# The last quarter of the attention steps: mixed tile, logits, value products, then the newer step's first head; on ScalarE the projection ahead of that head's copy

## The reference, cut to what matters

```
h = rms_norm(x, g_pre) * (1 + scale) + shift
p = h @ w_in            # indexer, retention (4 heads), gates, attention (8 query heads, 2 key/value heads)
mask: for each query the 256 best keys by an indexer's score (80 for the sample)
logits = q . k / 8, masked;  probs = softmax(logits);  o_a = probs @ v
mixed = concat(o_a * silu(gate_a), groupnorm(o_b) * silu(gate_b))
x = x + gate * rms_norm(mixed @ w_out, g_post)
```

## Time and profile before

| | us |
|---|---|
| median of 3 runs | 1493.13 (1491.31 to 1493.81) |
| profiled execution | 1492.05 |
| its span | 1490.2 |
| PE busy | 1392.9 (93%) |
| DVE busy | 1045.6 (70%) |
| ACT busy | 787.5 (53%) |
| POOL busy | 410.3 (28%) |

### The profile page before, as it was taken

One profiled execution on the slowest core, in us unless ns is written; L12 is line 12 of the kernel. 1 busy time (PEld: TensorE's weight loads), 2 busy tenths in 40 slices (PEclk: granted clock), 3 DMA queues, 4 the chain that ended last, 5 costly groups with the idle time before them and its releaser, 6 DMA issues.

```text
span 1490.2 us, 24410 instructions
## 1 busy us (share of the span) xinstructions
PE 1392.9 (93%) x7591; PEld 1060.5 (71%) x7591; DVE 1045.6 (70%) x3021; ACT 787.5 (53%) x1916; POOL 410.3 (28%) x360
## 2 busy tenths in 40 slices
PE   6779999999999999989996999999999999998997
PEld 1655777777887667657885677878887766765885
DVE  1697889999996556542287889999999655654225
ACT  2455666666325655654453566666631656656422
POOL 2551332433331001001188113433333101100100
PEclk9999999999999999999998999999999999999999
DMA  8422333423222112213252111211222211211324
GB/s 303 141 65 67 92 123 116 122 88 109 55 85 64 42 32 70 63 59 111 81 176 71 33 46 34 65 37 43 59 56 87 63 42 34 70 61 59 113 75 166
DMA packets 125191, 122.05 MB, mean 82 GB/s; under 512 B 33256, under 2 KB 94024, under 8 KB 125064
## 3 DMA queue, kind: packets, MB, share of 16 engines
q1 hardware_dynamic: 124608, 120.36, 26.7%
q10 hardware_dynamic: 456, 0.13, 0.0%
HBM read 93.55 MB, written 26.90 MB: 81 GB/s over the span
## 4 chain that ended last, share of the span: by engine, by line
PE 60%; DVE 27%; issue 5%; ACT 4%; DMA 2%; POOL 0%; DVEq 0%; ACTq 0%; SPq 0%; POOLq 0%
PE proj L944 12%; PE proj L945 12%; PE proj L947 11%; PE turn L923 8%; DVE U L1649 5%; PE logit L971 5%; PE out_bank L998 5%; DVE U L1839 2%; PE spare L971 2%; DVE by_cos_sin L1589 2%; DVE by_cos_sin L1587 1%; DVE probsT_more L1722 1%; DVE turned L1604 1%; DVE probsT_more L1724 1%; PE spare L909 1%
## 5 line engine op out<-in xcount | busy, mean ns | idle before, releaser
L944 PE MATMUL proj<-w_hi,h_hi 128*128 128x512 f32 (+2 forms) x1440 | 577.8, 401 | 3.6 <-POOL h_lo L1452 2.2
L945 PE MATMUL proj<-w_lo,h_hi 128*128 128x512 f32 (+2 forms) x1440 | 537.5, 373 | 0.0
L947 PE MATMUL proj<-w_hi,h_lo 128*128 128x512 f32 (+2 forms) x1280 | 479.6, 375 | 0.0
L1446 POOL TENSOR_TENSOR w_lo<-w_raw,w_hi 128x512 fp32r<-128x512 f32 (+2 forms) x160 | 206.7, 1292 | 788.8 <-ACT w_hi L1175 788.8
L944 PEld LDWEIGHTS proj<-w_hi,h_hi 128*128 128x128 f32 x1440 | 273.9, 190 | 63.0 <-issue 22.6
L945 PEld LDWEIGHTS proj<-w_lo,h_hi 128*128 128x128 f32 x1440 | 274.1, 190 | 31.0
L947 PEld LDWEIGHTS proj<-w_hi,h_lo 128*128 128x128 f32 x1280 | 242.1, 189 | 37.1
L1649 DVE TENSOR_SCALAR_CACHE_REDUCE U<-score,cand 128x384 bf16<-128x384 f32 x310 | 222.6, 752 | 2.2
L971 PE MATMUL logit<-keys,queries 64*128 64x512 f32 (+4 forms) x454 | 138.7, 548 | 14.2 <-ACT U L1306 10.9
L1286 ACT ACTIVATE probsT_more<-turn 128x512 f32<-128x512 f32 (+3 forms) x156 | 76.2, 492 | 120.8 <-PE turn L923 87.9
L923 PE MATMUL turn<-ident,U 128*128 128x128 f32 x672 | 110.1, 284 | 17.5 <-DVE h_lo L1851 8.8
(11 more groups left out here) (184 smaller groups left out, 2125.7 us busy)
## 6 DMA issues: line engine op xcount, KB each, us to landing
w_raw<-in_w_in_dram SPq DMA_DIRECT2D x80, 256.0 KB, 3.1
probsT_more<-in_w_ada_dram SPq DMA_DIRECT2D x64, 256.0 KB, 4.0
score<-mixed_dram SPq DMA_DIRECT2D x36, 256.0 KB, 2.8
score<-in_w_ada_dram SPq DMA_DIRECT2D x32, 256.0 KB, 5.3
w_raw<-in_w_out_dram SPq DMA_DIRECT2D x32, 256.0 KB, 3.4
U<-in_x_prompt_dram SPq DMA_DIRECT2D x14, 512.0 KB, 4.1
mixed_dram<-U SPq DMA_DIRECT2D x24, 192.0 KB, 2.1
gates_dram<-U SPq DMA_DIRECT2D x18, 256.0 KB, 2.2
```

What stands on the lines that cost most here:

```text
L944: nc.tensor.matmul(out, h_hi[:, k, tile], hi, start=(k == 0), stop=False)
L945: ins = nc.tensor.matmul(out, h_hi[:, k, tile], lo, start=False, stop=(t == SAMPLE and k == KT - 1))
L947: ins = nc.tensor.matmul(out, h_lo[:, k, tile], hi, start=False, stop=(k == KT - 1))
L1446: nc.gpsimd.tensor_tensor(w_lo[:, s % WS, 0:w], w_raw[:, n % RAWS, 0:w], w_hi[:, s % WS, 0:w].bitcast(F32), ALU.subtract).then_inc(w_lo_re ...
```

## The change

TensorE: with a mixed tile due, its two halves are turned at the start of the last quarter, in front of `middle`, and no longer after the quarters. In the last quarter of an attention step the order is then logits, value products of the older step, and only then the turns of the newer step's first head (both parts). Before, the first part of that head stood ahead of the logits, the last part behind them, the value products behind both. `plan_units` gets the same order of the banks. ScalarE: the mixed tile's high part is copied at the start of the last quarter; the first head's copy moves out of the quarter, behind the next step's projection. VectorE: `lower_mixed` moves up, directly behind the quarters. Nothing is computed otherwise than before. The diff:

```diff
--- before.py
+++ after.py
@@ -301,6 +301,8 @@
         if 0 <= i < STEPS and ada_group(i) is not None:
             turns.append(("ada", ada_group(i)))
         for q in range(QUARTERS):
+            if q == QUARTERS - 1 and mixed_turn(i):
+                turns += [("mix", *mixed_turn(i), u) for u in (0, 1)]
             logits += [("l", j, h, p) for h, p in dots_at(i, q)]
             if kind(j) == "ret" and q == 1:
                 logits += [("att", j), ("kv", j)]
@@ -314,8 +316,6 @@
                     turns.append(("q", i))
                 if has_cache_turn(i):
                     turns.append(("cache", i))
-        if mixed_turn(i):
-            turns += [("mix", *mixed_turn(i), u) for u in (0, 1)]
         for lt in hidden_turns(i):
             turns += [("h", *lt, u) for u in (0, 1)]
         if gate_spread(i):
@@ -1012,7 +1012,8 @@
                     turns.wait_taken(pe, ("q", g))
                     if t == SAMPLE:
                         turns.wait_taken(pe, ("cache", g - 1))
-                if att_head(g + 1, q, TURN_SLOT) is not None:
+                values_first = q == QUARTERS - 1
+                if att_head(g + 1, q, TURN_SLOT) is not None and not values_first:
                     turn_probs(att_head(g + 1, q, TURN_SLOT), False)
                 if dots_at(g + 1, q):
                     dot_keys(g + 1, q)
@@ -1026,10 +1027,12 @@
                     pe.wait_ge(k_dec_ready, RET[g] + 1)
                     logits.filled(nc.tensor.matmul(logits.bank(("kv", g))[:, 0:P], k_dec[:, RET[g] % 2, :],
                                                    rows[:, ROPE[g] % 4, 256:384], start=True, stop=True), ("kv", g))
-                if att_head(g + 1, q, TURN_SLOT) is not None:
-                    turn_probs(att_head(g + 1, q, TURN_SLOT), True)
                 if att_step(g + 1, q, VALUE_SLOT) is not None:
                     weigh_values(att_step(g + 1, q, VALUE_SLOT))
+                if att_head(g + 1, q, TURN_SLOT) is not None:
+                    if values_first:
+                        turn_probs(att_head(g + 1, q, TURN_SLOT), False)
+                    turn_probs(att_head(g + 1, q, TURN_SLOT), True)
                 if att_step(g + 1, q, BACK_SLOT) is not None:
                     turn_back(att_step(g + 1, q, BACK_SLOT))
 
@@ -1102,6 +1105,11 @@
                         turn_hidden(0, 1)
                     if q == 0:
                         late(i - 2)
+                    if q == QUARTERS - 1 and mixed_turn(i):
+                        l, t = mixed_turn(i)
+                        for u in (0, 1):
+                            pe.wait_ge(mixed_landed[u], 16 * (l * NT + t + 1))
+                            turn(("mix", l, t, u), [mixed[u][:, b * P:(b + 1) * P] for b in range(4)])
                     middle(i - 1, q)
                     if q == TURN_QUARTER and kind(i) in ("idx", "ret", "att"):
                         pe.wait_ge(rope_done, ROPE[i] + 1)
@@ -1113,11 +1121,6 @@
                         n = sum(1 for k in range(i + 1) if has_cache_turn(k))
                         pe.wait_ge(cache_landed, 32 * n)
                         turn(("cache", i), [cache_rows[:, b].rearrange("p s e -> p (s e)") for b in range(2)])
-                if mixed_turn(i):
-                    l, t = mixed_turn(i)
-                    for u in (0, 1):
-                        pe.wait_ge(mixed_landed[u], 16 * (l * NT + t + 1))
-                        turn(("mix", l, t, u), [mixed[u][:, b * P:(b + 1) * P] for b in range(4)])
                 for l, t in hidden_turns(i):
                     turn_hidden(l, t)
                 if gate_spread(i):
@@ -1307,7 +1310,7 @@
                         relu_count[0] += 1
                 if att_step(g + 1, q, COPY_SLOT) is not None:
                     copy_out(att_step(g + 1, q, COPY_SLOT))
-                if att_head(g + 1, q, TURN_SLOT) is not None:
+                if att_head(g + 1, q, TURN_SLOT) is not None and q < QUARTERS - 1:
                     take_probs(att_head(g + 1, q, TURN_SLOT))
                 n = att_head(g + 1, q, EXP_SLOT)
                 if n is not None:
@@ -1388,6 +1391,14 @@
                         late(i - 2)
                         if 0 <= i < STEPS and tested_bit(i) is not None:
                             test_bit(i)
+                    if q == QUARTERS - 1 and mixed_turn(i):
+                        l, t = mixed_turn(i)
+                        act.wait_ge(proj_done, step_of(l, OUT0 - 1, t) + 1)
+                        for u in (0, 1):
+                            key = ("mix", l, t, u)
+                            turns.wait_full(act, key)
+                            nc.scalar.activation(high_half(t, u), by_slice(turns.bank(key)[:], t),
+                                                 ACT.Copy).then_inc(mix_hi_ready, 1)
                     middle(i - 1, q)
                     if q == TURN_QUARTER and kind(i) in ("idx", "ret", "att"):
                         take_turn(i)
@@ -1403,6 +1414,8 @@
                     nc.scalar.activation(ada_row, spare[:], ACT.Copy).then_inc(ada_copied, 1)
                 if i + 1 < STEPS:
                     take_projection(i + 1)
+                if att_head(i, QUARTERS - 1, TURN_SLOT) is not None:
+                    take_probs(att_head(i, QUARTERS - 1, TURN_SLOT))
                 for l, t in hidden_turns(i - 1):
                     if l:
                         split_hidden(l, t)
@@ -1410,14 +1423,6 @@
                     l, c, t = lct(i)
                     act.wait_ge(x_new, l * NT + t + 1)
                     square_x(x_ordinal(l, t))
-                if mixed_turn(i):
-                    l, t = mixed_turn(i)
-                    act.wait_ge(proj_done, step_of(l, OUT0 - 1, t) + 1)
-                    for u in (0, 1):
-                        key = ("mix", l, t, u)
-                        turns.wait_full(act, key)
-                        nc.scalar.activation(high_half(t, u), by_slice(turns.bank(key)[:], t),
-                                             ACT.Copy).then_inc(mix_hi_ready, 1)
                 if gate_spread(i):
                     l, s = gate_spread(i)
                     if s == 0:
@@ -1978,6 +1983,8 @@
                         finish_attention(att_step(i, q, BACK_SLOT))
                     if q == 2 and kind(i - 2) == "ret":
                         measure_retained(i - 2)
+                if mixed_turn(i):
+                    lower_mixed(*mixed_turn(i))
                 if i + 1 < STEPS and lct(i + 1)[2] == SAMPLE:
                     sum_sample(i + 1)
                 for n in passes_here[half:]:
@@ -1997,8 +2004,6 @@
                     l, t, lo, hi = roots_first(i)
                     if lo == 0:
                         add_residual(l, t, unit)
-                if mixed_turn(i):
-                    lower_mixed(*mixed_turn(i))
                 for l, t in hidden_turns(i):
                     if l == 0:
                         take_hidden(l, t)
```

## The result

The changed kernel takes 1470.53 us (median of 4 runs, 1468.03 to 1473.56), the kernel before beside it 1493.47; the ratio is 0.9832 [0.9812, 0.9853], about 23 us less. A second measurement, on another occasion (e9), gave 1470.94 against 1493.9, ratio 0.9849 [0.9829, 0.987]. The forecast was 1471.7.

A forecast was written before the change was run, and what follows sets the result against it. TensorE was taken as the bound, with about 10 us of short waits per layer. 17.4 - 0.4 + 2.6 + 1.0 + 0.8 = 21.4 us off 1492.05 gives 1470.65; with 1.08 for the median, 1471.7, range 1465 to 1482.

The forecast's parts named there:

- (a): Attention steps: head after values, projection before its copy; removes 8.7 us of TensorE waits per layer, 17.4 in two, 0.4 new.
- the 0.75: A TensorE wait at 549.02 for ScalarE's copy of turned probabilities, of which 0.25 us was left standing.
- the new wait of 0.2: Mixed tile's second half directly behind the query turn, one step per layer: 0.2 us each, 0.4 in all.
- ScalarE's stand behind the products: ScalarE waits behind the value products seven times per layer, 16.1 us, throwing ScalarE and VectorE some 3 us back.
- the mixed tile's 4.4: TensorE's waits for the mixed tile's low half, 4.4 us per layer; all to go with its earlier turn.
- (b): Last quarter of 16 steps with two-part keys: three tile-shape changes instead of four, 0.16 each, 2.6 us saved.
- (c): Pure output steps: ScalarE copies the mixed tile ahead of the projection; gate spread waits 0.5 less, 1.0 us in two layers.
- (d): Queues the mixed tile moves past: loads still land in time, ScalarE's 1.3 us wait in the sample step costs nothing.
- (e): TensorE's clock fall in layer 2 costs 1.5 us; half, 0.8, taken as gain, ends 0 and 1.5.
- The slack of 0.3 us: First head's copy in the long step is done by 544.0; TensorE wants its bank at 544.3.

The follow-up runs named there:

- e9: The changed kernel again, unaltered, measured on another occasion: 1470.94 us, ratio 0.9849 to the kernel before.
- e1: Kernel before, with only ScalarE's order changed: it copies the newer step's first head behind the next projection. 1479.59 us, ratio 0.9902 to the kernel before.
- e2: Kernel before, with only TensorE's order changed: first head turned behind the value products. 1505.12 us, ratio 1.007 to the kernel before.
- e4: Changed kernel, with the first head's first part turned between logits and value products. 1495.24 us, ratio 1.0008 to the kernel before.
- e5: Changed kernel, with the mixed tile at its old place and the first head's first part turned ahead of the value products. 1476.86 us, ratio 0.9872 to the kernel before.
- e6: Changed kernel, with ScalarE's copy of the first head later, behind the next step's weight split and result copy. 1470.46 us, ratio 0.9835 to the kernel before.
- e7: Changed kernel, with the value products ahead of the logits in the last quarter. 1509.09 us, ratio 1.0088 to the kernel before.
- e3: Changed kernel, with the mixed tile back at its old place on all three engines. 1475.3 us, ratio 0.9869 to the kernel before.
- e8: Changed kernel, with the gate spread one step later. 1468.84 us, ratio 0.9816 to the kernel before.
- e10: Changed kernel with the gate spread one step later, measured again beside the unaltered changed kernel. 1468.68 us, ratio 0.9825 to the kernel before.

## Why the prediction was right

- *(a) waits, 17.4 less 0.4 new.* Measured per layer: 10.1 became 1.6 (without the gate spread), 8.5, in two 17.0. Right, and nearly place by place: of the 0.75, 0.47 stayed and not 0.25, and of the new wait of 0.2 there is none in the list. That the waits hang on ScalarE's stand behind the products is shown by e1 (remove that alone, 6.6 us of stretch). e2, in which exponential and projection come no earlier in the long steps and later in the one-part steps, fits it with 4.9 more. What was not right is the division: ScalarE's order alone already took the mixed tile's 4.4 down to 0.4 (e1), and its own move then brought 2.6 by other waits.
- *(b) shape changes, 2.6.* The quarter from projection to projection takes 536.88 to 543.19, 6.31 us, where it took 6.48 (536.68 to 543.16): 0.17. The other steps of this kind without a mixed tile and without a wait give the same (491.91 to 496.15, where it is 495.82 to 499.89 now); taken for all 16 it is 2.7. Logits to values costs no more than logits to turn, 0.52 from the last logits' start (538.64) to the first product. e4 and e5 give 0.14 and 0.15. The drain that the Trainium skill states (TensorEngine Tiling (Array Packing), Key Properties) shows here as that much at turn to values; behind logits no run shows it, since the 0.52 is what lies between one pair of logits and the next as well (538.11 to 538.64).
- *(c) gate spread, 1.0.* 1.21 became 0.65, 1.1 in two layers.
- *(d) queues.* No wait for a mixed load, and none of the sample's chain at TensorE.
- *(e) the clock, 0.8 taken, 1.5 the end.* The stretch of layer 2 was 1.6 us longer than that of layer 1 and is now equal: 1.6. This is one execution of the kernel before; how often the fall comes in others isn't known.

Sum 17.0 + 2.7 + 1.1 + 1.6 = 22.4, against 25.0 measured in the stretches. One-part steps give some of the missing 2.6: their last quarter and the next take 3.79 us (579.91 to 583.70) where they took 3.84 (580.30 to 584.14), about 0.05 in 20 steps, 1.0. The rest is what the list of waits leaves out. This quarter has the same instructions before (first pair) and after (second pair), but for the wait:

```profile
637.83 0.47 PE L944 MATMUL proj<-w_hi,h_hi 128*128 128x512 f32 x1
...
641.37 0.63 PE L923 MATMUL turn<-ident,U 128*128 128x128 f32 x4 [1.91 <-DVE h_lo L1851]
...
643.30 0.47 PE L944 MATMUL proj<-w_hi,h_hi 128*128 128x512 f32 x1
```

```profile
634.70 0.48 PE L944 MATMUL proj<-w_hi,h_hi 128*128 128x512 f32 x1
...
638.07 0.47 PE L944 MATMUL proj<-w_hi,h_hi 128*128 128x512 f32 x1
```

It went from 5.47 to 3.37 us, 2.10 less for a wait listed as 1.91. The list counts from the modelled end of the product before (0.40 us long here), while in a stream the next one starts 0.23 behind its start. Another quarter with a wait of 1.40 gives 1.58 (658.67 to 663.51, now 653.12 to 656.38). Over all quarters that lost a wait this is some 1.4 us per layer. Some 0.6 is lost again where the mixed tile stands now: the quarter from 614.50 to 620.77, 5.86 us without its wait, takes 6.04 (613.35 to 619.39) with none listed. That leaves 0.8 per layer, the 1.6 in two that the sum lacks.

That the forecast of 1471.7 lies within 1.2 us of the measured 1470.53 is in part luck. The gain was forecast 3.6 us too small (21.4 against 25.0), and the kernel before, whose 1493.13 was the median of three executions, takes 1495.56 by all 37. The two errors offset each other. The mechanism and the size of its main term don't hang on that.

The slack of 0.3 us given for the head's copy was wrong, on the careful side (e6): it is 0.7, and I overlooked ScalarE's idle time of 1.0 ahead of the copy. What decides is whether the products outlast exponential and projection, which e7 turns round.

## What to carry to other kernels

An instruction that waits for a slow neighbour should stand behind what has no such wait on its engine, as long as it still comes in time for whoever waits for it; look for the engine's longest repeated wait even where that engine is half idle, and follow what is queued behind it to the bound engine. Reordering the bound engine helps only after that, and reordering it alone can lose (e2). When a turn is moved in a ring of two banks, check who releases the bank that it will meet, and what that release waits for in turn (e4, e7).

## What the runs showed of the hardware

TensorE's granted clock fell inside an attention stretch seven times in twelve profiles, each time at a wait or right behind one. Its mean in five of these places, of e2, e4 (two) and e7 (two), is the third number from the end of each line:

```profile
1246.00:1249.50 3.50, 3.50 (x15) 2.50 (x12) 2.21 (x8) 1.56 (x3) 0.00 (x0) 0.59 0.03 5
```

```profile
1340.00:1343.50 3.50, 3.50 (x22) 1.90 (x18) 1.23 (x4) 0.60 (x1) 0.00 (x0) 0.59 0.05 9
1361.00:1367.00 6.00, 6.00 (x30) 3.47 (x31) 0.20 (x1) 0.95 (x3) 0.00 (x0) 0.52 0.00 0
```

```profile
665.80:669.20 3.40, 3.40 (x12) 2.71 (x11) 0.00 (x0) 1.80 (x4) 1.28 (x1) 0.52 0.00 0
1338.50:1342.00 3.50, 3.48 (x16) 3.24 (x18) 1.90 (x5) 1.25 (x5) 0.00 (x0) 0.57 0.07 16
```

The waits ahead of them end at 1245.21 (1.24 us), 1338.17 (2.55), 1360.74 (2.82), 664.95 (2.82) and 1338.52 (2.28). The other two are the kernel before, behind the wait of 1.91 that ends at 1346.39, and e7 from 1359.6 (0.65 over 3.4 us), behind one of 2.55 that ends at 1357.71. Waits as long passed without a fall (2.81 at 655.09 in e4; rope's 1.7 ahead of every stretch). In the 16 stretches of the eight other profiles (e1, e3, e5, e6, e8 to e10 and the changed kernel), with no wait longer than 1.22 us inside, it didn't fall once. So a wait of TensorE here costs its length (and up to 0.2 us that the list leaves out, as above), and in some executions 1.5 us or more on top, the time that the lower level, 1.2 GHz, takes from it; in e4 the second layer's stretch is 4.6 us longer than the first's with the same waits. This was seen beside the edits, not tested by itself.
